# C loaded once and copied by GpSimd; the decays of layer 1 spread by DMA and masked by GpSimd instead of added by a product of ones

## The reference, cut to what matters

```python
# layer 0, S5 group: C enters as two real matrices, (64 groups, 16, 64) each
y = einsum('blgp,ghp->blgh', hr, c_re) - einsum('blgp,ghp->blgh', hi, c_im)
...
# layer 1, per head: c is a running sum over the tokens of the log of the forget gate
logf = log_sigmoid(f_logit + b_f)
c = cumsum(logf, axis=1)
s = einsum('bhqd,bhkd->bhqk', q, k) * scale
s = s + c[q position] - c[k position]
s = where(causal, s, -inf)
p = softmax(s);  y = p @ v
```

## Time and profile before

| | |
|---|---|
| median of 3 runs | 972.98 us (972.85 to 974.23) |
| the profiled execution's own time | 973.47 us |
| its span in the profile | 971.8 us |
| granted TensorE clock, mean | 1.00 of full speed |
| busy share: PE, DVE, ACT, POOL | 99%, 64%, 61%, 9% |
| moved by DMA | 164.14 MB, mean 169 GB/s |

### The profile page before, as it was taken

One profiled execution on the slowest core, in us unless ns is written; L12 is line 12 of the kernel. 1 busy time (PEld: TensorE's weight loads), 2 busy tenths in 40 slices (PEclk: granted clock), 3 DMA queues, 4 the chain that ended last, 5 costly groups with the idle time before them and its releaser, 6 DMA issues.

```text
span 971.8 us, 14450 instructions
## 1 busy us (share of the span) xinstructions
PE 957.5 (99%) x5267; PEld 821.7 (85%) x5267; DVE 623.9 (64%) x986; ACT 594.6 (61%) x988; POOL 90.4 (9%) x92
## 2 busy tenths in 40 slices
PE   8989999999999999999999999999999999999998
PEld 7978888888888999888888888888888888888887
DVE  5578889799799864755555565546455555555553
ACT  5589878969969765644555555456545644565332
POOL 2101002002020000000102200220021002200000
PEclk9999999999999999999999999999999999999999
DMA  8876444435334347465899976667999856644662
GB/s 285 198 181 195 153 131 130 131 110 170 116 127 142 119 137 277 162 220 182 163 176 169 175 180 163 185 175 154 166 163 168 195 170 179 184 155 156 214 216 86
DMA packets 115937, 164.14 MB, mean 169 GB/s; under 512 B 21301, under 2 KB 56234, under 8 KB 115626
## 3 DMA queue, kind: packets, MB, share of 16 engines
q1 hardware_dynamic: 99504, 159.67, 62.1%
q10 hardware_dynamic: 16378, 3.74, 1.9%
HBM read 161.29 MB, written 2.10 MB: 168 GB/s over the span
## 4 chain that ended last, share of the span: by engine, by line
PE 94%; DVE 2%; ACT 1%; ACTq 1%; issue 1%; DMA 1%; SPq 0%
PE bank L456 24%; PE bank L458 24%; PE bank L457 24%; PE bank L483 3%; PE bank L484 3%; PE bank L485 3%; PE bank L715 1%; PE bank L698 1%; PE bank L526 1%; PE bank L601 1%; ACTq L1141 1%; PE bank L682 1%; PE bank L592 1%; PE bank L705 1%; PE bank L614 1%
## 5 line engine op out<-in xcount | busy, mean ns | idle before, releaser
L958 DVE TENSOR_TENSOR wl<-raw,wh 128x1024 fp32r<-128x1024 f32 x295 | 361.9, 1230 | 273.5 <-ACT wh L950 271.3
L950 ACT ACTIVATE wh<-raw 128x1024 fp32r<-128x1024 f32 x295 | 310.4, 1058 | 170.8 <-PE bank L458 118.3
L456 PE MATMUL bank<-wh,xh 128*128 128x512 f32 x768 | 309.8, 403 | 4.3 <-DVE wl L958 4.3
L458 PE MATMUL bank<-wh,xl 128*128 128x512 f32 x768 | 300.8, 392 | 0.0
L457 PE MATMUL bank<-wl,xh 128*128 128x512 f32 x768 | 299.6, 390 | 0.0
L456 PEld LDWEIGHTS bank<-wh,xh 128*128 128x128 f32 x768 | 144.6, 188 | 32.0 <-DVE wl L958 5.6
L458 PEld LDWEIGHTS bank<-wh,xl 128*128 128x128 f32 x768 | 144.2, 188 | 31.4
L457 PEld LDWEIGHTS bank<-wl,xh 128*128 128x128 f32 x768 | 144.9, 189 | 26.8
L456 PE MATMUL bank<-wh,yh 128*128 128x512 f32 x256 | 100.7, 393 | 0.0
L458 PE MATMUL bank<-wh,yl 128*128 128x512 f32 x256 | 99.9, 390 | 0.0
L457 PE MATMUL bank<-wl,yh 128*128 128x512 f32 x256 | 99.8, 390 | 0.0
(11 more groups left out here) (327 smaller groups left out, 1108.6 us busy)
## 6 DMA issues: line engine op xcount, KB each, us to landing
raw<-in_o_w_in SPq DMA_DIRECT2D x128, 512.0 KB
raw<-in_e_w_in SPq DMA_DIRECT2D x130, 256.0 KB, 3.4
raw<-in_e_w_out SPq DMA_DIRECT2D x32, 512.0 KB
raw<-in_o_w_out SPq DMA_DIRECT2D x32, 512.0 KB
raw<-in_e_w_in SPq DMA_DIRECT2D x31, 512.0 KB
raw<-in_s_w_glu SPq DMA_DIRECT2D x8, 512.0 KB
res<-in_x SPq DMA_DIRECT2D x8, 256.0 KB, 6.3
res<-in_x SPq DMA_DIRECT2D x1, 2048.0 KB, 8.3
```

The lines of the kernel that those rows point to most:

```text
L456: nc.tensor.matmul(o, l_hi, w_hi, start=first, stop=False)
L458: mm = nc.tensor.matmul(o, l_lo, w_hi, start=False, stop=last)
L950: nc.scalar.activation(wh[:, j % RING, :], raw[:, j % RING, :], ACT.Copy).then_inc(hi_done, 1)
L958: nc.vector.tensor_tensor(wl[:, j % RING, :], raw[:, j % RING, :], wh[:, j % RING, :].bitcast(F32), ALU.subtract).then_inc(lo_done, 1)
```

## The change

C is loaded once instead of twice: ACT issues four loads instead of six, at positions 0, 2, 4 and 6 of the second chunk, and POOL copies each half of `c_n` beside itself (two copies of 128 x 512) once all four have landed. `c_turn` on PE waits for that copy.

In layer 1 the products of ones, `nck`, `nks`, `sel` and `fox_keys` are gone. ACT writes `nct` (16 x 256) to a buffer in DRAM, waits for it, and reads it back in four loads of four heads each, spread over all 128 partitions into `decay` (512 KB each, 4 KB of source). POOL adds the causal mask to `decay` with two additions of 128 x 128 for each head, 32 in all: two heads between the norms of q and of k, the other fourteen behind them. DVE reads `decay` where it read `mask`. Ahead of the loop over groups 1 to 3 DVE waits for all sixteen heads. Small tiles move to other places in `scr` to make room.

```diff
@@ -231,16 +231,16 @@
         main1 = used["scr"]
 
         used["scr"] = main0
+        decay = carve("scr", FOX_GROUPS * FOX_HEADS, 3 * P)
+        used["scr"] = main0
         x1_st = [carve("scr", NT, CW) for _ in range(2)]
+        used["scr"] = main0 + FOX_GROUPS * FOX_HEADS * 3 * P
         sq = carve("scr", 2, CW)
         wf = lamv.rearrange("p a b -> p (a b)").rearrange("p (k n) -> p k n", k=KT)
         f_sb = carve("scr", T, parts=32)
         nct = carve("scr", T, parts=16)
-        nks = carve("scr", T)
-        sel = carve("scr", 16)
-        c_sb = carve("scr", NT, 16)
-        ls = carve("scr", NT, 16)
-        lsa = carve("scr", NT, 16)
+        assert used["scr"] <= main1
+        c_sb, ls, lsa = (vz[:, 0, 32 * k:32 * k + 32].rearrange("p (t n) -> p t n", t=NT) for k in range(3))
         used["scr"] = main0
         glu_s = carve("scr", CT, T)
         used["scr"] = 0
@@ -267,8 +267,6 @@
         with nc.sbuf_tensor("mg", [P, TB, NCH], F32) as mg:
             pass
         wf2 = sb("wf2", [P, KT, 32], F32R)
-        nck = wf2.rearrange("p a b -> p (a b)").rearrange("p (h t) -> p h t", h=2)
-        ones_r = sb("ones_r", [P, P], F32R)
         phr = sb("phr", [P, GP], F32R)
         ph_hi, ph_lo, mag_all, ph_all = (phc[:, k, 0:GP] for k in range(4))
 
@@ -322,7 +320,9 @@
             ("qkt_ps", "qkt_sb", "sc_ps", "sc_max", "p_exp", "p_ready", "pt_ps", "pt_sb"))
         pv_ps, pv_ssq, pv_rn, y_ready, yt_ps, yt_hi, yt_lo = (sem(n) for n in
             ("pv_ps", "pv_ssq", "pv_rn", "y_ready", "yt_ps", "yt_hi", "yt_lo"))
-        fox_b, fox_cq, c_split = sem("fox_b"), sem("fox_cq"), sem("c_split")
+        rows_out, decay_done, fox_cq = (sem(n) for n in ("rows_out", "decay_done", "fox_cq"))
+        decay_in = [sem(f"decay_in{k}") for k in range(FOX_GROUPS)]
+        decay_rows = nc.dram_tensor("decay_rows", (FOX_GROUPS * FOX_HEADS, T), F32).ap()
         glu_half = sem("glu_half")
         glu_sig, glu_y0, glu_y, glu_hi, glu_lo, silu_done = (sem(n) for n in
             ("glu_sig", "glu_y0", "glu_y", "glu_hi", "glu_lo", "silu_done"))
@@ -596,12 +596,9 @@
             def fox_scores(i, h):
                 pe.wait_ge(qkt_sb, fox_no(i, h) + 1)
                 pe.wait_ge(sc_max, fox_score(i, h))
-                pe.wait_ge(fox_b, FOX_HEADS * i + (h + 1))
                 for o, t, w in ((0, 1, T), (T, 0, P)):
-                    nc.tensor.matmul(scb[:, o:o + w], qkt[:, h % 2, 0, t * P:(t + 1) * P],
-                                     qkt[:, h % 2, 1, 0:w], start=True, stop=False)
-                    mm = nc.tensor.matmul(scb[:, o:o + w], ones_r[:, :], nck[:, h % 2, 0:w],
-                                          start=False, stop=True)
+                    mm = nc.tensor.matmul(scb[:, o:o + w], qkt[:, h % 2, 0, t * P:(t + 1) * P],
+                                          qkt[:, h % 2, 1, 0:w], start=True, stop=True)
                 mm.then_inc(sc_ps, 1)
 
             def fox_p_turn(i, h):
@@ -768,7 +765,7 @@
             def c_turn(k):
 
                 if k == 0:
-                    pe.wait_ge(s5_in, 16 * 6)
+                    pe.wait_ge(c_twice, 1)
                     pe.wait_ge(prm_ang, 1)
                     pe.wait_ge(rbc_done, 1)
                 for e in range(CT // 2):
@@ -980,8 +977,8 @@
                       for at, name in ((0, "s5_b_re"), (1, "s5_b_im"))]
             small += [(lamv[:, k, :], bc(d[name][0], 64), bc_in) for k, name in
                       enumerate(("da_lambda_q1", "da_lambda_k1", "da_lambda_q2", "da_lambda_k2"))]
-            matrices += [(c_n[:, at, :, g, :], d[name][0].rearrange("(a b) h p -> (b h) a p", b=8), s5_in)
-                      for at, name in ((0, "s5_c_re"), (1, "s5_c_im")) for g in range(2)]
+            matrices += [(c_n[:, at, :, 0, :], d[name][0].rearrange("(a b) h p -> (b h) a p", b=8), s5_in)
+                      for at, name in ((0, "s5_c_re"), (1, "s5_c_im"))]
 
             def tiles_up(b):
 
@@ -1136,8 +1133,8 @@
                         if 5 <= j < 5 + NT:
                             squares(j - 5)
                     else:
-                        if j < 6:
-                            dst, src, arrived = matrices[j]
+                        if j % 2 == 0:
+                            dst, src, arrived = matrices[j // 2]
                             act.dma_start(dst, src).then_inc(arrived, 16)
                         params(c, j)
                         if j >= 3:
@@ -1424,6 +1421,17 @@
                     act.wait_ge(c_ps, 1)
                     nc.scalar.activation(c_sb, yb[:, 64:96].rearrange("p (a b) -> p a b", a=2), ACT.Copy).then_inc(c_done, 1)
                     nc.scalar.mul(nct, yb[0:16, 128:384], -1.0).then_inc(c_done, 1)
+                if s == 13:
+                    act.wait_ge(c_done, 2)
+                    act.wait_ge(x1_kept, 4)
+                    act.dma_start(decay_rows, nct).then_inc(rows_out, 16)
+                if s == 14:
+                    act.wait_ge(rows_out, 16)
+                if s in (14, 18, 22, 26):
+                    n = (s - 14) // 4
+                    heads = slice(FOX_HEADS * n, FOX_HEADS * (n + 1))
+                    act.dma_start(decay[:, heads, 0:T], decay_rows[heads, :].rearrange("(a h) t -> a h t", a=1)
+                                  .to_broadcast([P, FOX_HEADS, T])).then_inc(decay_in[n], 16)
 
             for s in range(FOX_UNITS):
                 split_hi(act, CH_FOX + s // UNITS, s % UNITS + LEAD)
@@ -1566,7 +1574,7 @@
                 link(v.tensor_tensor(pi[:, 3, :], n, a, ALU.add))
 
             def b_blocks():
-                dve.wait_ge(s5_in, 16 * 6)
+                dve.wait_ge(s5_in, 16 * 4)
 
                 def wide(x):
                     return x.rearrange("p (a b) -> p a b", b=1).to_broadcast([P, GP, 16])
@@ -1874,23 +1882,23 @@
                 link(v.tensor_reduce(ssn[:, m:m + 4], sq[:, t, :].rearrange("p (s e) -> p s e", e=HD), AX.X, ALU.add))
                 v.tensor_scalar(ssn[:, m:m + 4], ssn[:, m:m + 4], 1.0 / HD, EPS, ALU.mult, ALU.add).then_inc(qk_ss, 1)
 
-            def fox_keys(i, h):
-                dve.wait_ge(sc_ps, fox_score(i, h) - 1)
-                if isinstance(i, int) and i == 0 and h == 0:
-                    dve.wait_ge(c_split, 1)
-                v.tensor_scalar(nck[:, h % 2, :], nks, sel[:, bass.ds(FOX_HEADS * i + h, 1)], None, ALU.mult)\
-                    .then_inc(fox_b, 1)
-
             def fox_score_in(i, h):
                 dve.wait_ge(sc_ps, fox_score(i, h) + 1)
                 if h == 0:
                     dve.wait_ge(pt_ps, fox_no(i, 0))
                 dve.wait_ge(fox_cq, FOX_HEADS * i + (h + 1))
+                if isinstance(i, int):
+                    dve.wait_ge(decay_done, FOX_HEADS * i + (h + 1))
                 c = 2 * (h % 2)
-                v.scalar_tensor_tensor(out=s_sb[:, h, 0:T], in0=mask[:, 0:T], scalar=cq[:, c + 1:c + 2],
-                                       in1=scb[:, 0:T], op0=ALU.add, op1=ALU.add)
-                link(v.scalar_tensor_tensor(out=s_sb[:, h, T:T + P], in0=mask[:, T:T + P], scalar=cq[:, c:c + 1],
-                                            in1=scb[:, T:T + P], op0=ALU.add, op1=ALU.add))
+                at = bass.ds(FOX_HEADS * i + h, 1)
+
+                def one(x):
+                    return x.rearrange("p (a n) -> p a n", a=1)
+
+                v.scalar_tensor_tensor(out=one(s_sb[:, h, 0:T]), in0=decay[:, at, 0:T], scalar=cq[:, c + 1:c + 2],
+                                       in1=one(scb[:, 0:T]), op0=ALU.add, op1=ALU.add)
+                link(v.scalar_tensor_tensor(out=one(s_sb[:, h, T:T + P]), in0=decay[:, at, T:T + P], scalar=cq[:, c:c + 1],
+                                            in1=one(scb[:, T:T + P]), op0=ALU.add, op1=ALU.add))
                 v.tensor_reduce(nmax[:, 2 * h:2 * h + 1], s_sb[:, h, T:T + P], AX.X, ALU.max, negate=True)
                 v.tensor_reduce(nmax[:, 2 * h + 1:2 * h + 2], s_sb[:, h, 0:T], AX.X, ALU.max, negate=True).then_inc(sc_max, 1)
 
@@ -1918,8 +1926,6 @@
                     fox_squares(i, 0, s - UNITS - 1)
                 if s in (2 * UNITS + 1, 2 * UNITS + 2):
                     fox_squares(i, 1, s - 2 * UNITS - 1)
-                if s in FOX_QKT:
-                    fox_keys(i, FOX_QKT[s])
                 if s in FOX_SC:
                     fox_score_in(i, FOX_SC[s])
 
@@ -2012,15 +2018,6 @@
                 if s == 10:
                     dve.wait_ge(f_abs, 2)
                     v.tensor_scalar(lsa, lsa, 1.0, None, ALU.add).then_inc(f_exp1, 1)
-                if s == 14:
-
-                    link(v.memset(nks, 0.0))
-                    v.tensor_copy(ones_r[:, :], ones)
-                    v.tensor_tensor(sel, ident[:, 0:16], ident[:, 32:48], ALU.add)
-                    dve.wait_ge(c_done, 2)
-                    link(v.tensor_copy(nck[0:16, 0, :], nct))
-                    v.tensor_copy(nks[0:16, :], nck[0:16, 0, :].bitcast(F32))
```

(13 more changed lines are left out.)

4 lines of the change are left out of this document (2 added, 2 removed).

## The result

| | before | after |
|---|---|---|
| median | 972.91 us (972.63 to 974.23, 6 runs) | 965.83 us (964.85 to 968.69, 6 runs) |
| ratio | | 0.9927, 95% interval 0.9913 to 0.994 |
| the profiled execution's own time | 973.47 us | 964.85 us |
| its span | 971.8 us | 963.1 us |

The changed kernel is 7.1 us faster. The profiled execution, the fastest of its six, is 8.6 us faster than that of before, which is not the fastest of its six. Of all the executions behind this document one, of `e5_behind`, ran at a granted clock of 0.75 of full speed (1185.66 us) and is left out.

What follows compares the result with a forecast made beforehand. PE, busy 957.5 of 971.8 us, was taken as the bound. 4.0 us from the scores plus 4.2 from the early stall, less 0.1 for copies, gave 8.1: median 972.98 to 964.9 us, range 963.4 to 968.6.

Steps and rivals of the forecast that it cites:

- the forecast's own range: Whole kernel: 963.6 to 966.2 us if no rival happens, chance 0.62.
- The scores: Layer 1, PE's 16 heads: without the products of ones each takes 1.11 instead of 1.36 us, 4.0 us saved.
- The early stall: PE's waits for `wl` ahead of units 17 to 19: 5.0 us shrink to 0.8, 4.2 us gained.
- c_re held until about 51.5: ACT's queue, second chunk: c_re, issued at about 49.5, still waits for b_im's pieces until about 51.5.
- The copies: POOL's two copies of C during DVE's `b_factors`: cost DVE between nothing and 1.2 us, taken as 0.1.
- The decays: Layer 1, store, decay loads and POOL's mask additions ahead of the norms of k: mostly hidden, taken as 0 us.
- The first rival: First head of layer 1: first decay load lands late, norms of k and PE wait, 967 to 968 us; chance 0.2.
- the forecast's own signs: Profile signs: scores 1.11 us, casts near 45 and 53, under 1.5 us lost ahead of units 17-19, no L592 wait near 542.
- The sentence beside that rival: DMA engines take queues in turn by packet, so the decay load's 32 pieces an engine each let a weights packet by.
- The weights: Layer 1, decay loads delay weights by 6, at worst 12 us; PE's 5.9 us lead covers it, taken as 0.
- The sum: Whole kernel: 4.0 + 4.2 - 0.1 = 8.1 us saved, median 972.98 to 964.9 us.
- The low end: Range's fast end: 4.2 for the scores and 5.0 for the stall, 963.6, set at 963.4 us for error.

Runs made afterwards that it cites:

- e5_behind: Changed kernel with all 32 mask additions of POOL behind the norms of k; 965.51 us, ratio 0.9922.
- e6_sums_first: Changed kernel with DVE's sums of squares of k ahead of the subtraction at slots 10 and 18 of each group; 966.34 us, ratio 0.9929.
- e10_late_wait: Changed kernel, mask additions behind norms of k, ACT's store wait and first decay load at slot 16 instead of 14; 966.53 us, ratio 0.9926.
- e11_best: Changed kernel with late store wait, mask additions behind norms of k, and sums of squares ahead of the subtraction; 965.97 us, ratio 0.9928.
- e13_all: Changed kernel with C loaded ahead of B, late store wait, additions behind norms, sums of squares ahead of the subtraction; 965.81 us, ratio 0.9918.
- after_again: The changed kernel itself, unedited, run and profiled once more in a later series; 967.69 us, ratio 0.9935.
- e1_c_once: Kernel before with only the C part: C loaded once, four spaced loads, POOL copies, products of ones kept; 970.37 us, ratio 0.9968.
- e9_small: Changed kernel with each decay load bringing 16 of 256 columns, the rest zeroed by POOL; 966.07 us, ratio 0.9927.
- e4_apart: Kernel before, C still loaded twice, its six loads set apart at positions 0, 2, 4, 5, 6, 7, no POOL copy; 969.21 us, ratio 0.9955.
- e3_close: Changed kernel with its four loads in a row at positions 0 to 3; 970.08 us, ratio 0.9973.
- e12_c_first: Changed kernel with C loaded ahead of B: c_re, c_im, b_re, b_im at positions 0, 2, 4, 6; 967.29 us, ratio 0.9937.
- e2_decays: Changed kernel with the six C and B loads of before and no POOL copy, so the decays part alone; 972.37 us, ratio 0.9994.

## Why the prediction was right

The median came out at 965.83 us, 0.9 above the 964.9 predicted and inside the forecast's own range. Its steps one by one:

**The scores, 4.0 us.** Right in mechanism and size. 1.36 became 1.11 us, and where nothing else is lost the second distance shrank by 3.9 to 4.1 us in four kernels (`e6_sums_first`, `e10_late_wait`, `e11_best`, `e13_all`). The same sequence without the products of ones, was the right row to price it from.

**The early stall, 4.2 us, 0.8 left.** Right. In the seven kernels that issue B first with room (after, after_again, e1, e6, e9, e10, e11) the first distance is on average 0.94 us above 8.25, from 0.20 to 1.41. That agrees with the 0.8 partly by luck: up to 0.9 us of it are the copies, which the sum had at 0.1, and without them (`e4_apart`) nothing is left. The forecast "c_re held until about 51.5" was the right thing to ask for: it got through between 50.0 and 52.3. In the profiled execution it was 50.0, the cast of unit 16 began at 51.42 and not at 52.9, and DVE's chain ended at 67.66 where 68.9 was expected. The reason given was right too, that the order on ACT's queue matters and not the 512 KB; `e3_close` and `e4_apart` show it from both sides.

**The copies, 0.1 us.** Undersized, and this is the term of the sum that was. The range "between nothing and 1.2 us" was right, the value taken from it was not. POOL and DVE of after:

```profile
58.32 1.23 POOL L2127 COPY scr<-scr 128x512 f32<-128x512 f32 x2 [17.98 <-DMA scr<-in_s_c_im]
...
58.55 0.50 DVE L1540 TENSOR_TENSOR scr<-scr 128x32 f32<-128x32 f32 x1
```

Two copies of 0.6 us held one DVE operation for 0.3 us here (0.50 instead of 0.19). That is the least of nine profiles: in `e12_c_first` and most others two operations were held for 0.3 to 0.4 each, and DVE's chain became 0.3 to 0.9 us longer than the 14.8 of the kernels without a copy in it. In after_again, 0.75 of the 1.26 us of stall ahead of unit 19 are theirs. The full 1.2 us of the rule of the Trainium skill ("SBUF — State Buffer", "SBUF: two separate sides") was not paid in any of them. In kind the rule is borne out, by operations that aren't copies: DVE with two SBUF inputs is held, and where POOL is the one that comes second it is POOL that stands still (an addition of 0.46 us took 1.52 beside the subtraction L955).

**The decays, 0 us.** This is the step that was too kind. It priced the landing of the load, the additions and the bytes, and not what it had named itself, "a wait for the store, beside an ACT that is 61% busy". What stands behind that wait on ACT are the casts. The store took 4.8 to 7.4 us, against the 2 to 4.7 of the estimate, and a chain that leads to PE goes from the casts over DVE's sums of squares to the norms. The chain over the load, the one that was priced, came close behind: in after the additions were done at 534.83 and the sums at 534.89. The four additions had taken 2.8 us there, not the 1.5 of the estimate, because one of them met a subtraction of DVE. In after_again, `e3_close` and `e12_c_first` POOL then waited 0.6 us for DVE's sums, in `e2_decays` and `e9_small` 2.0.

What it cost PE at the first head differs: no wait is shown in after, `e3_close` and `e9_small`, 0.2 us in after_again, 1.5 in `e12_c_first`, 2.5 and the half clock behind it in `e2_decays`, and none in the four kernels that cut the chain at either end. The norms' 1.9 us to spare went down to 0.2 in after. The first rival, a stall at the first head, thus happened in part, by another way than the one described: the first load landed 4.1 to 4.8 us after its issue in the six profiles where POOL waited for it, at the short end of what was expected. By the forecast's own signs after passes, and after_again, with its wait on POOL ahead of L592 at 544.37, does not quite. The sentence beside that rival takes each of the 32 pieces for a packet of its own, and no run here shows how many pieces go between two turns.

**The weights, 0 us.** Right in size for PE, which in after never waited for `wl` in layer 1, wrong in what makes them late. The estimate was about bandwidth; `e9_small` and `e10_late_wait` show that it is mostly ACT's hold. In `e6_sums_first` ACT waited 10.1 us for weights and PE lost nothing.

**The third group.** The second distance of after is 0.7 us above 894.7, that of after_again and of `e9_small` 1.0. Of this 0.5, 0.4 and 0.7 us are a wait of PE for the norms in the third group, at 735 to 739 us, and not at the first head. It looks like a consequence of the change and isn't shown to be one: the last load of `decay` landed at 570.6, ACT waited for weights from 700 to 745 us in the kernel before too (6.4 us in all; 9.3 in `e1_c_once` and 11.4 in `e4_apart`, against 8.8 in after), and with the layer 1 of before the norms ended 0.2 us (before) and 0.1 us (`e4_apart`) ahead of PE there. The three kernels with the sums of squares first have no such wait.

**The sum.** 8.1 us were forecast, and the span of the profiled execution is 8.7 us shorter: 4.84 from unit 16 to 19, 3.3 behind, and 0.55 ahead of unit 16, where the arrival of the first inputs differs from execution to execution. The medians differ by only 7.1, because the profiled execution is the luckiest of its six. after_again, whose profile has 1.3 us of the early stall and 1.0 of the late ones, is the other measure: 967.69, 6.3 us below its series and 2.8 above the forecast. Both lie inside the stated 963.4 to 968.6, but that the first median came within 0.9 us of 964.9 owes something to luck. The low end is also mis-added: 4.2 and 5.0 off the median of 972.98 give 963.8, not 963.6.

**What stays open.** The two parts alone give 2.8 us (`e1_c_once`, 973.2 to 970.37) and 0.8 us (`e2_decays`, to 972.37), together 3.7, and both at once 7.1 or 6.3. The missing 3 us are accounted for in the profile of `e2_decays` by the 4.3 us of its second distance. It stays open why its store should take 7.4 us when the six loads of the second chunk, 470 us earlier, and the missing copies are the only differences. `e3_close`, just as late at unit 19, had 4.9 us and nearly no stall. One profile a kernel doesn't settle it. The edits against the late stall (`e6_sums_first`, `e10_late_wait`, `e11_best`) do what they should in their profiles, and their medians, 965.97 to 966.53, are no lower than the 965.83 of after. A kernel with the spaced loads, C loaded twice and no copy, together with the decays, was not run; 0.9 us better is an estimate, from the first distances of `e1_c_once` and `e4_apart`. Nor were two of the six executions of after, at 968.2 and 968.7 us, profiled.

## What to carry to other kernels

An engine that issues DMAs and also computes pays for an issue twice: while the queue is full, and while it waits for one DMA to land before it issues the next. So before such an issue or wait is placed, list what is queued behind it; loads with many small pieces go last or far apart, and a store that is to be read back gets some slots before anyone waits for it (three, of 2.75 us each, were enough here). Copies moved to POOL are free only while DVE has time to spare: here they fell into the one chain that PE waited for. And where a chain runs from a cast over a subtraction to a norm to PE, take out of it what doesn't depend on its predecessor: the sums of squares only stood behind a subtraction by the order of the code.

## What the runs showed of the hardware

- A load of 256 KB in 4096 pieces of 64 bytes keeps the issues behind it from going through: with two of them in front, the next load was let through 12.5 to 13.5 us after the first of them was issued, in ten of eleven profiles, whether it came one slot or three behind. With the two C loads in front and B's loads 5.8 us apart, all four issues took 0.37 to 0.44 us.
- PE's granted clock fell from 1.00 to 0.50 of full speed behind an idle stretch of 2.5 us (`e2_decays`) and stayed there for some 3 us, which cost 1.6 us more than the idle stretch itself. Behind idle stretches of 1.2 to 1.6 us it stayed at 1.00.
- Loads of 512 KB, spread from 4 KB of source over 128 partitions, landed 4.0 to 13.0 us after their issue. Where ACT had waited for the store, the first took 4.0 to 4.7 us and the others 7.1 to 11.8.
- A store of 16 KB to DRAM took 4.8 to 7.4 us from issue to landing beside a full stream of weights. The Trainium skill, "DMA: Bandwidth & Descriptors", "Anatomy of one DMA — SWDGE (gpsimd) path", gives a DMA issued by GpSimd a fixed cost of about 2 us, mostly the confirmation of the write, and says it can be surprisingly long for a target in HBM; these stores were issued by ACT and took more than twice that.
- An addition of 128 x 128 on POOL took 0.46 us, and up to 1.52 when it met DVE's subtraction of 128 x 1024 (1.23 us, two SBUF inputs). Two copies of 128 x 512 on POOL (0.6 us each) made a chain of short DVE operations 0.3 to 0.9 us longer.
